# Loading a mixture of experts in halves: 82 more weight units of 4 MB are split in two, and the last two are cut by rows

## What is computed

```python
def expert_block(args):
    xb, e = args
    gu = xb @ w_gate_up[e] + b_gate_up[e]          # (1024) x (1024, 2048)
    gate, up = gu[:, :D_EXPERT], gu[:, D_EXPERT:]
    gate = jnp.minimum(gate, SWIGLU_LIMIT)
    up = jnp.clip(up, -SWIGLU_LIMIT, SWIGLU_LIMIT)
    act = (up + 1.0) * (gate * jax.nn.sigmoid(SWIGLU_ALPHA * gate))
    return act @ w_down[e] + b_down[e]             # (1024) x (1024, 1024)
```

## Time and profile before

| | |
|---|---|
| runs before | 1357.94 us median, 1357.71 to 1358.34 |
| the profiled execution | 1358.47 us, its span 1356.8 us |
| TensorE busy | 1318.4 us (97% of the span) |
| VectorE, ScalarE, GpSimd busy | 417.3, 258.0, 35.6 us |
| memory read | 477.33 MB |
| mean granted clock of TensorE | 0.996 |

### The profile page before, as it was taken

The page is one execution under the profiler, slowest core; times in us unless marked ns, Lnnn a source line. Parts: engine busy times, 40 slices in busy tenths (PEclk is TensorE's granted clock), DMA queues, the critical chain, the costliest instruction groups (busy, mean ns, idle before and its releaser), DMA issues.

```text
span 1356.8 us, 16732 instructions
## 1 busy us (share of the span) xinstructions
PE 1318.4 (97%) x6850; PEld 728.7 (54%) x6850; DVE 417.3 (31%) x1089; ACT 258.0 (19%) x583; POOL 35.6 (3%) x56
## 2 busy tenths in 40 slices
PE   9999999999999999999999999999999999999997
PEld 8888888888887344344443443334334333434433
DVE  3755557885312221212111212112111112212112
ACT  2113374484202111010110110101011010101102
POOL 0000012110000000000000000000000000000000
PEclk9999999999999999999999999999999999999999
DMA  9445449997998999999999999999999999999995
GB/s 253 151 131 159 153 148 273 309 344 252 264 333 337 373 425 418 431 431 431 430 430 431 432 431 427 431 431 432 429 430 431 430 430 431 431 432 429 431 424 206
DMA packets 94709, 489.37 MB, mean 361 GB/s; under 512 B 8673, under 2 KB 73761, under 8 KB 78873
## 3 DMA queue, kind: packets, MB, share of 16 engines
q1 hardware_dynamic: 84896, 460.21, 84.0%
q0 software_dynamic: 4608, 24.41, 5.2%
q10 hardware_dynamic: 5129, 3.66, 1.0%
HBM read 477.33 MB, written 11.19 MB: 360 GB/s over the span
## 4 chain that ended last, share of the span: by engine, by line
PE 71%; DMA 27%; ACTq 0%; DVE 0%; issue 0%; ACT 0%; POOL 0%; SPq 0%; POOLq 0%; DVEq 0%
PE bank L320 70%; DMA plain_conv<-in_w_down 9%; DMA ring<-in_w_down 9%; DMA ring<-in_w_gate_up 6%; DMA plain_conv<-in_w_gate_up 3%; PE bank L971 2%; ACTq L691 0%; ACTq L689 0%; DVE exn L2022 0%; ACT plain_conv L937 0%; ACT ring L695 0%; ACT plain_conv L685 0%; SPq L377 0%; DVE exn L1555 0%; DVE plain_conv L2025 0%
## 5 line engine op out<-in xcount | busy, mean ns | idle before, releaser
L320 PE MATMUL bank<-ring,plain_conv 128*64 128x512 f32 (+1 forms) x1312 | 297.6, 594 | 13.9 <-DMA ring<-in_w_gate_up 13.7
L320 PE MATMUL bank<-exn,ring 128*128 128x264 f32 (+1 forms) x1168 | 262.2, 388 | 0.2 <-DVE exn L1555 0.2
L320 PEld LDWEIGHTS bank<-exn,ring 128*128 128x128 f32 (+1 forms) x1168 | 217.4, 189 | 40.3 <-issue 3.2
L320 PEld LDWEIGHTS bank<-ring,plain_conv 128*64 128x64 f32 (+1 forms) x1312 | 92.3, 137 | 190.3 <-issue 166.1
L320 PE MATMUL bank<-plain_conv 128*64 128x512 f32 (+2 forms) x848 | 185.3, 586 | 9.2 <-DMA plain_conv<-in_w_gate_up 8.8
L320 PE MATMUL bank<-ring,exn 128*64 128x512 f32 x576 | 127.6, 595 | 1.9 <-DMA ring<-in_w_down 1.9
L320 PEld LDWEIGHTS bank<-plain_conv 128*64 128x64 f32 (+2 forms) x848 | 59.3, 138 | 125.2 <-issue 109.0
L1950 DVE TENSOR_TENSOR xT<-xT,bank 128x264 f32<-128x264 f32 x128 | 54.4, 429 | 216.1 <-PE bank L320 214.4
L1956 DVE TENSOR_SCALAR bank<-bank 128x512 f32<-128x512 f32 x31 | 21.7, 700 | 321.1 <-PE bank L320 321.1
L320 PE MATMUL bank<-plain_conv,exn 128*64 128x512 f32 (+1 forms) x422 | 99.9, 590 | 2.1 <-DMA plain_conv<-in_w_down 1.8
L874 ACT ACTIVATE exn<-bank 128x512 f32<-128x512 f32 x31 | 18.5, 598 | 414.7 <-DVE bank L1956 414.7
(11 more groups left out here) (299 smaller groups left out, 842.0 us busy)
## 6 DMA issues: line engine op xcount, KB each, us to landing
ring<-in_w_gate_up SPq DMA_DIRECT2D x35, 4096.0 KB, 39.7
plain_conv<-in_w_gate_up SPq DMA_DIRECT2D x23, 4096.0 KB, 40.2
ring<-in_w_down SPq DMA_DIRECT2D x16, 4096.0 KB, 40.4
plain_conv<-in_w_down SPq DMA_DIRECT2D x11, 4096.0 KB, 39.0
ring<-in_w_in SPq DMA_DIRECT2D x36, 1024.0 KB, 5.4
ring<-in_w_gate_up SPq DMA_DIRECT2D x8, 2048.0 KB, 12.0
ring<-in_w_proj_b SPq DMA_DIRECT2D x8, 1024.0 KB, 9.9
plain_conv<-in_w_gate_up SPq DMA_DIRECT2D x4, 2048.0 KB, 12.5
```

The source lines that it names most:

```text
L320: return nc.tensor.matmul(out, w, x, start=start, stop=stop)
```

## The change

Units 3 to 93 are all split now, so units 11 to 92 (82 of them) become two DMAs of 2 MB in place of one of 4 MB, in both the written-out pairs and the loop. Each half waits for its own half of the place, and TensorE has one more wait in the middle of each unit. Units 94 and 95 come in four pieces of two rows each (8 KB per partition, 1 MB), in the order: rows 0 and 1 of both, 2 and 3 of both, 4 and 5 of both, 6 and 7 of both. The last down products follow that order, with both column halves for each piece; only the last piece is still done a column half at a time.

```diff
-SPLIT = range(3, 11)
-HALVES = [sum(n % PLACES == q for n in (*SPLIT, 93)) for q in range(PLACES)]
+SPLIT = range(3, 94)
+ROWS_EACH = (48, 48, 32)
+HALVES = [sum(n % PLACES == q for n in SPLIT) for q in range(PLACES)]
...
-        columns_landed = [sem(f"columns_landed{i}") for i in range(2)]
+        rows_landed = [sem(f"rows_landed{i}") for i in range(3)]
...
-            def load_pair(p, m, q, first=0, split=(), final=False):
+            def load_pair(p, m, q, final=False):
 
                 j = PLACES * m + q
-                for c in range(first, UNITS):
+                for c in range(UNITS):
                     n = (q + c) % PLACES
                     used = 2 * UNITS * PAIRS * p + 2 * UNITS * j + 2 * (c - PLACES)
-                    if c in split or final and c == 3:
-                        for h in range(2):
-                            sp.wait_ge(S["w_used"], used + 1 + h)
-                            second = half_landed[n]
-                            load_half(j, c, n, h, second if h else unit_landed[n])
+                    if final and c >= 4:
+                        sp.wait_ge(S["w_used"], used + 2)
+                        load_rows(j, c, n, 0, 2, unit_landed[n])
                         continue
+                    sp.wait_ge(S["w_used"], used + 1)
+                    load_half(j, c, n, 0, unit_landed[n])
                     sp.wait_ge(S["w_used"], used + 2)
-                    if final and c >= 4:
-                        load_half(j, c, n, 0, unit_landed[n])
-                    else:
-                        load_unit(j, c, n)
+                    load_half(j, c, n, 1, half_landed[n])
                 if final:
-                    for h in range(2):
+                    for r in range(1, 4):
                         for c in (4, 5):
-                            load_columns(j, c, (q + c) % PLACES, h, columns_landed[h])
+                            load_rows(j, c, (q + c) % PLACES, 2 * r, 2 * r + 2, rows_landed[r - 1])
...
                     n = UNITS * q + c
-                    if isinstance(m, int) and m == 0 and n in SPLIT:
-                        half_arrived(n % PLACES, 1 + sum(o % PLACES == n % PLACES for o in SPLIT if o < n))
-                    if final and c == 3:
-                        half_arrived(3, HALVES[3])
+                    if isinstance(m, int) and m == 0 and n < SPLIT[0]:
+                        return
+                    half_arrived(n % PLACES, UNITS * m + n // PLACES + (n % PLACES >= SPLIT[0]))
...
-                down_both(range(4), range(2), lambda x: arrived(4 + x))
-                down_both(range(4, KT), [0], columns_of(0)).then_inc(S["y_half"], 1)
-                down_both(range(4, KT), [1], columns_of(1)).then_inc(S["w_used"], 4)
+                down_both(range(2), range(2), lambda x: arrived(4 + x))
+                for r in (1, 2):
+                    down_both(range(2 * r, 2 * r + 2), range(2), rows_of(r))
+                down_both(range(6, KT), [0], rows_of(3)).then_inc(S["y_half"], 1)
+                down_both(range(6, KT), [1], rows_of(3)).then_inc(S["w_used"], 4)
```

More of the change, by code:

```diff
@@ L385, in load_rows @@
                 sp.dma_start(unit[n][:, D * r0:D * r1], unit_of(j, c)[:, r0:r1, :].rearrange("p s n -> p (s n)")).then_inc(landed, 16)
-            def load_columns(j, c, n, h, landed):
-                dst = unit[n][:, HALF:BIG].rearrange("p (s n) -> p s n", s=4)
-                sp.dma_start(dst[:, :, 512 * h:512 * h + 512], unit_of(j, c)[:, 4:8, 512 * h:512 * h + 512]).then_inc(landed, 16)
             for w, k in ((a["w_proj_a"], KT), (a["w_proj_b"], 2 * KT), (a["w_out"], KT)):
@@ L446, in load_pairs @@
                 sp.wait_ge(S["w_used"], 2 * UNITS * PAIRS * p + 1)
-                load_rows(0, 5, 0, 2, 4, columns_landed[0])
+                load_rows(0, 5, 0, 2, 4, rows_landed[0])
                 sp.wait_ge(S["half_used"], 3 * p + 2)
@@ L450, in load_pairs @@
                 sp.wait_ge(S["w_used"], 2 * UNITS * PAIRS * p + 2)
-                load_rows(0, 5, 0, 6, 8, columns_landed[1])
-                load_pair(p, 0, 1, split=range(5))
-                for q in range(2, PLACES):
+                load_rows(0, 5, 0, 6, 8, rows_landed[1])
+                for q in range(1, PLACES):
                     load_pair(p, 0, q)
@@ L1380, in down @@
                         if first and x and s == 2:
-                            pe.wait_ge(columns_landed[0], 48 * p + 16)
+                            pe.wait_ge(rows_landed[0], 48 * p + 16)
                         if s == 4:
@@ L1384, in down @@
                         if first and x and s == 6:
-                            pe.wait_ge(columns_landed[1], 48 * p + 16)
+                            pe.wait_ge(rows_landed[1], 48 * p + 16)
                         for half in range(2):
@@ L1400, in down_both, with rows_of @@
                     return ins
-                def columns_of(half):
+                def rows_of(r):
                     def landed_of(x):
-                        pe.wait_ge(columns_landed[half], 48 * p + 48)
+                        pe.wait_ge(rows_landed[r - 1], ROWS_EACH[r - 1] * (p + 1))
                         return unit[(q + 4 + x) % PLACES]
```

## The result

The changed kernel takes **1362.12 us** (median of 8 runs, 1360.69 to 1363.74) against 1358.12 us before in the same comparison (8 runs, 1357.48 to 1359.27): **4.0 us slower**, a ratio of 1.0027 with a 95% interval of 1.0018 to 1.0036. Repeated on another chip beside later kernels it was 1361.88 against 1358.34 us, 3.5 us slower, ratio 1.0029 (1.0018 to 1.0041). The forecast was 1362.3.

What follows compares the result with a forecast made beforehand. The DMA stream, with TensorE's work behind its last deliveries, was taken to set the end. 5.3 - 0.3 - 0.6 = +4.4 us gave 1362.9 us for the profiled execution, 1362.3 for the median; range 1358.8 to 1364.8.

Steps and rivals of the forecast that it cites:

- What bounds the kernel: Whole run: a DMA stream that hardly pauses, 9.717 us a unit; TensorE works off a backlog, then waits for it.
- Term 1: Units 11 to 92 in the stream: two halves take 0.065 us more than a whole unit, +5.3 us at unit 92.
- Term 2: Units 92 and 93: second halves land at 1316.6 and 1326.4, TensorE waits at 93, first down product moves to about 1335.0.
- Term 3: Last 8 MB: eight 1 MB pieces take 19.8 us instead of 20.1, the last landing at 1346.2; -0.3 us.
- Term 4: Behind the last piece: 8 products take 3.5 us in both kernels, 0.6 us of idle time is used up; -0.6 us.
- Halves that cost nothing: Rival on the stream: halves cost it nothing, TensorE waits for the last piece, 0.9 us earlier than now, 1357.0; chance 0.12.
- The clock drop: Rival at the end: TensorE slows after waits at 93 and the last pieces, up to 1.7 us more, 1364.0; chance 0.10.
- The delays: Rival on the stream: irregular delays fall differently, one of 1.5 us more or less, 1360.8 or 1363.8; chance 0.12.
- Costed at nothing: Split units: 82 more TensorE waits and 82 more SyncE issues of 0.33 us cost nothing; first column half's copy still done first.

Runs made afterwards that it cites:

- experiment 2: Kernel before with only the last two down units in row pieces and their products in that order, units 11 to 92 whole: 1357.80 against 1358.40 us.
- experiment 4: Changed kernel with units 11 to 92 cut into even and odd partitions, two DMAs with 32 KB runs: 1358.80 against 1358.18 us for the kernel before.
- experiment 1: Changed kernel with the last two down units loaded and multiplied as before, the 82 units in halves alone: 1363.42 against 1358.40 us for the kernel before.
- experiment 5: Kernel before with units 11 to 92 each one DMA of two 16 KB runs per partition from two places: 1363.79 against 1358.40 us.
- experiment 6: Kernel before with units 11 to 92 each one DMA of four 8 KB runs per partition from four places: 1376.13 against 1358.18 us.
- experiment 3: Changed kernel with units 11 to 92 cut into partitions 0 to 63 and 64 to 127, two DMAs with 32 KB runs: 2186.96 us, ratio 1.6102.
- the second version: Kernel before with unit 92 split, row pieces, and rows 6 and 7 of the last two units as single pieces: 1356.35 against 1358.18 us; repeated, -0.1.

## Why the prediction was right, and where it was off

**What bounds the kernel.** This held. The stream has no hole before or after, and splitting the middle units changed TensorE's waits but not their sum: between 850 and 1350 us those for loads were 26.2 us in 27 waits before, the longest 2.7, and are 26.4 us in 32 waits, the longest 1.5. From TensorE's waits in that stretch of the changed kernel:

```profile
PE bank L321 <- DMA ring<-in_w_gate_up: 12.6, 13, 1.5
PE bank L321 <- DMA plain_conv<-in_w_gate_up: 8.5, 10, 1.3
PE bank L321 <- DMA ring<-in_w_down: 4.2, 7, 1.1
PE bank L321 <- DMA plain_conv<-in_w_down: 1.1, 2, 0.6
```

**Term 1, +5.3 forecast.** Undisturbed, a unit went from 9.715 to 9.788, 0.073 in place of the forecast 0.065: 6.0 us over 82 units. From the end of unit 10 to that of unit 92 the two profiles differ by 4.9 us (803.8 before, 808.8 after). The rest is in the delays that the forecast called irregular: what the landings fall behind their median spacing adds up to 7.2 us before and 6.1 after. The other traces agree. The same stretch took 804.7 us in experiment 2 and 804.6 in experiment 4, both with runs of 32 KB, and 808.7 in experiment 1 and in the second profile of the change. So the stream lost 4.0 to 4.9 us, not 6.0. With one DMA of short runs (experiment 5) it took 810.2.

These delays are not irregular. Before, landings come 1.0 to 1.1 us late at units 23, 43, 61 and 81 and 0.4 to 0.6 late at 18, 39, 59 and 75; after, 1.2 to 1.4 late at 18, 38, 58 and 75. The other traces have the same pattern: in every 16 to 21 units there is one delay of 1.2 to 1.9 us, or two that add up to as much. Over the 82 units the sum is 6.1 to 8.5 us in the traces of the two kernels and experiments 1, 2, 4, 5 and 6. What they are is open. That their sum would not change was a guess, and it was 1 to 2 us off.

That the forecast's 0.065 came out so near was luck. It rests on nine halves that took 44.0 us. In the changed kernel's profile they took 44.4 (461.2 to 505.6), but in eight of the thirteen profiles other than that of experiment 3 it was 45.2 to 45.6 us, as a delay falls into it (experiment 4: from 460.1 to 505.4). From such a trace the same working gives about 10.07 us a unit and a loss near 29 us. The median of the nine single spacings is 4.89 us a half in both traces: it hardly depends on where a delay falls.

The forecast named the price but not its cause: it counted DMAs and their halves in term 1, runs in term 3. Experiments 4, 5 and 6 settle it for the runs. Two DMAs with long runs cost nothing that can be told, one DMA with short runs costs all, and runs of half that length cost three times as much. The Trainium skill's sentence that on trn2 the semaphore's write is essentially free ("DMA: Bandwidth & Descriptors", Anatomy of one DMA — SWDGE (gpsimd) path) is borne out by experiment 4. What did not follow from it is that halves are free. The Trainium skill's overhead of about 3 cycles per packet ("DMA: Bandwidth & Descriptors", Why small descriptors are slow), with the same page's 850 MHz, gave an estimate of 28 ns a unit. The measurement decides: 8 more runs on each of 16 engines take 74 ns, 9 ns each and not 3.5.

**Term 2.** Unit 92's second half was forecast for 1316.6 and landed at 1314.4. Unit 93's was forecast 5.3 us later than before and came 3.1 later (1324.15): 1.8 of the difference is the earlier start of the stream, 0.4 that term 1 was 4.9 in this trace. The wait before it, forecast, is there with 1.33 us.

**Term 3, eight pieces in 19.8 us.** From 1324.15 to 1343.91 it is 19.76.

**Term 4.** TensorE was to come to the last group 0.8 us ahead of the landing; it waited 0.56 us, with 8 products behind, 3.6 us where 3.5 was forecast. The copy of the first column half was in time. The slack of 0.6 us is what the halves alone lost as well. In the two profiles the last group moved by 2.2 us (1341.87 to 1344.05) and not by the 4.4 of the sum: 4.9 of the stream, 0.9 less for what follows unit 92, as forecast, and 1.8 less for the start. That the median came within 0.2 us of the forecast is partly luck: the two comparisons gave +4.0 and +3.5 for a sum of +4.4.

**The rivals.** Halves that cost nothing: excluded, ratio 1.0027 with 1.0018 as the lower end. The clock drop: not in the last pairs of either profile of the change; it was seen at unit 87 before the change, and also behind the 2.7 us wait at 1204.4, absorbed both times, and at unit 88 in the second profile of the second version, where it was not absorbed. The delays: single executions of the change scatter by 3 us (1360.69 to 1363.74); how much of it is theirs and how much the start of the stream, the single profiles don't tell.

**Costed at nothing.** 82 waits on TensorE, 82 issues on SyncE: experiment 4 has both and shows 0.6 us, not told from none. The forecast left open whether the queue would be full; at the end it was, with issues of 3.4 to 4.2 us, and the last eight pieces still came in the 19.8 us that were forecast.

Not tried: whether the run's price is one of reading or of writing, what the recurring delays are, and what makes the start of the stream scatter by 3 us.

## What to carry to other kernels

Where a stream of loads saturates the DMA engines to the end, ask first what a change does to the length of the contiguous runs, since every run has its price (9 ns on its engine here) and the number of DMAs of 2 MB has none to speak of. Split a load only where the consumer's early start reaches the end of the kernel, here the last few units, and even there the gain was 0 to 1.8 us, at the edge of what can be told; the other splits bought nothing and cost 4 to 5 us. And a chain of waits that ends in a DMA of 40 us whose neighbours land every 9.7 us names the queue, not the issue; compare the spacing of landings, which showed 0.7% that busy shares (1.00 and 1.01) hide. Take the median of many spacings, not the distance of two landings: a delay of 1 us between the two is as large as the price of 14 units.

## What the runs showed that I had not expected

- A DMA of 2 MB into partitions 0 to 63, or 64 to 127, moves 212 GB/s; into the even or the odd 64 it moves 431. The engines are equally busy in both. The kernel took 1.61 times as long.
- Issues of SyncE that blocked for 6 to 10 us (46 of the 82 in experiment 6) left the stream as fast as its runs allow.
- Unit 6's first half lands anywhere from 460.1 to 463.5 us in executions of kernels that are equal up to there, nearly as much scatter as the whole effect of the change; the difference could only be read behind it.
- Delays in the landings, 1.2 to 1.9 us in one or in two pieces, come back every 16 to 21 units.
